# Routing block by block inside the mixer, and new distances between the operands of wide products

## The reference

```
h  = LN0(concat(meta, x))
p  = h @ w_in                  # q,k,v | conv B,C,h | two gates
y  = (g_a * (attention @ w_attn_out) + g_c * (conv @ w_conv_out)) @ w_o
h1 = LN1(alpha*h + y)
g  = top-1 of 4 groups by h1 @ w_rg + b_rg              # softmax over groups
e1, e2 = top-2 of the 8 experts of that group by h1 @ w_re + b_re
weight = g_top * softmax(e_top)
ffn = sum over the 2 experts of weight * (silu(x @ w_gate) * (x @ w_up)) @ w_down
out = LN2(alpha*h1 + ffn)      # meta rows dropped
```

## Time and profile before

| | us |
|---|---|
| median of 3 runs | 4279.54 (4263.64 to 4280.54) |
| profiled execution, its own time | 4267.06 |
| its span | 4265.2 |
| mixer's last wide matmuls end, last router rows begin | about 2634 |
| route, first to last VectorE instruction | 2666.09 to 2744.40 |
| first wide matmul of the experts | 2758.32 |

### The profile page before, as it was taken

One profiled execution on the slowest core, in us unless ns is written; L12 is line 12 of the kernel. 1 busy time (PEld: TensorE's weight loads), 2 busy tenths in 40 slices (PEclk: granted clock), 3 DMA queues, 4 the chain that ended last, 5 costly groups with the idle time before them and its releaser, 6 DMA issues. The chain is left out here.

```text
span 4265.2 us, 60440 instructions
## 1 busy us (share of the span) xinstructions
PE 4144.7 (97%) x20152; PEld 3426.1 (80%) x20153; DVE 2023.0 (47%) x2942; ACT 1433.5 (34%) x2594; POOL 694.2 (16%) x983
## 2 busy tenths in 40 slices
PE   8999999999999999999999998599999999999997
PEld 7888888888888888888888887388788888888886
DVE  3554333433433433433433433677756566765664
ACT  2421311311311311311311310466646465655563
POOL 2000000000000000000000000233333343333333
PEclk9999999999999999999999999799999999999999
DMA  8787355455455455455455454377656566765562
GB/s 249 237 298 244 139 197 211 144 193 209 142 197 204 151 194 197 162 187 194 163 193 190 169 187 178 129 244 253 240 186 217 185 211 224 255 209 194 195 211 90
DMA packets 274310, 839.18 MB, mean 197 GB/s; under 512 B 46128, under 2 KB 95280, under 8 KB 222528
## 3 DMA queue, kind: packets, MB, share of 16 engines
q1 hardware_dynamic: 226080, 715.43, 48.2%
q0 software_dynamic: 48096, 121.71, 8.5%
HBM read 717.47 MB, written 177.21 MB: 210 GB/s over the span
## 5 line engine op out<-in xcount | busy, mean ns | idle before, releaser
L896 PE MATMUL bank<-hT_hi,w_slot 128*128 128x512 f32 x2176 | 861.8, 396 | 7.8 <-DVE w_slot L712 7.1
L897 PE MATMUL bank<-hT_lo,w_slot 128*128 128x512 f32 x2176 | 849.2, 390 | 0.0
L898 PE MATMUL bank<-hT_hi,w_slot 128*128 128x512 f32 x2176 | 848.6, 390 | 0.0
L1652 PE MATMUL e_bank<-e_w_hi,e_xT_hi 128*128 128x512 f32 x1312 | 522.4, 398 | 11.9 <-DVE e_xT_lo L1578 10.6
L1654 PE MATMUL e_bank<-e_w_hi,e_xT_lo 128*128 128x512 f32 x1312 | 514.7, 392 | 0.0
L1653 PE MATMUL e_bank<-e_w_lo,e_xT_hi 128*128 128x512 f32 x1312 | 514.1, 392 | 0.0
L1583 DVE TENSOR_TENSOR e_w_lo<-e_raw,e_w_hi 128x1024 fp32r<-128x1024 f32 x384 | 443.9, 1218 | 118.4 <-ACT e_w_hi L1534 118.4
L896 PEld LDWEIGHTS bank<-hT_hi,w_slot 128*128 128x128 f32 x2176 | 409.0, 188 | 107.2 <-issue 24.1
L898 PEld LDWEIGHTS bank<-hT_hi,w_slot 128*128 128x128 f32 x2176 | 409.0, 188 | 87.3
L897 PEld LDWEIGHTS bank<-hT_lo,w_slot 128*128 128x128 f32 x2176 | 409.3, 188 | 81.8
L1534 ACT ACTIVATE e_w_hi<-e_raw 128x1024 fp32r<-128x1024 f32 x376 | 366.2, 1054 | 0.0
(11 more groups left out here) (275 smaller groups left out, 6496.0 us busy)
## 6 DMA issues: line engine op xcount, KB each, us to landing
w_slot<-split_weights SPq DMA_DIRECT2D x353, 1024.0 KB, 4.8
e_raw<-in_w_exp_gate_dram SPq DMA_DIRECT2D x128, 512.0 KB, 5.9
e_raw<-in_w_exp_up_dram SPq DMA_DIRECT2D x128, 512.0 KB, 6.1
e_raw<-in_w_exp_down_dram SPq DMA_DIRECT2D x128, 512.0 KB, 5.4
split_weights<-w_slot SPq DMA_DIRECT2D x50, 1024.0 KB, 5.9
h_rows<-h_rows SPq DMA_DIRECT2D x64, 512.0 KB, 7.9
x_rows<-in_x_dram SPq DMA_DIRECT2D x32, 512.0 KB, 5.4
raw<-in_w_in_dram SPq DMA_DIRECT2D x30, 512.0 KB, 7.6
```

The source lines that it names most:

```text
L896: pe.matmul(out, hi, x_hi, start=first, stop=False)
L897: pe.matmul(out, hi, x_lo, start=False, stop=False)
L898: return pe.matmul(out, lo, x_hi, start=False, stop=last)
L1652: pe.matmul(out_p, hi, x_hi, start=first, stop=False)
```

## The change

**Routing.** The steps of `route` become functions over 4 tiles (`choose_group`, `choose_first`, `choose_second`, `weigh`, `rank_rows`, `count_up_to`, `place_rows`). In each of blocks 1 to 7 the mixer runs them for the block before, at six places in the strips. GpSimd scatters 8 x 128 records of 8 bytes (row code and weight) into a DRAM tensor `slot_records`, in which every expert has its own region. The tensor is cleared in block 0 by one DMA. After the mixer, `route` does the same for the last block's 4 tiles alone, works out the tile ranges, lists only the last block's 8 x 128 choices by one-hot products, gathers the rest by one indirect DMA of one record row per tile, transposes it and adds the two. Tables (`ident`, `before`, `ones`, `desc`, ...) are made once at the start.

**Distances.** `line_up` puts unused bytes ahead of tensors so that `hT`, `oT`, `zT` and `mixT` start at 256 modulo 512 and `w_slot` at 0. In the experts, 64 unused bytes stand between `e_rows` and `e_xT`, so that `e_xT` and `e_aT` start 64 after `e_w_hi` and `e_w_lo` modulo 512.

```diff
-def mixer(nc, t, x, w_in, w_attn_out, w_conv_out, w_o, h1, logits):
+def mixer(nc, t, x, w_in, w_attn_out, w_conv_out, w_o, h1, tb, records):
...
+        def line_up(name, residue=0):
+            gap = (residue - nc.sbuf_base) % LINE
+            if gap:
+                sb("gap_" + name, [P, gap // 4])
...
+        line_up("hT", HALF)
         hT_hi = sb("hT_hi", [P, KD, TOK], F32R)
...
+        line_up("oT", HALF)
         oT_hi = sb("oT_hi", [P, KA, TOK], F32R)
...
+        line_up("arena", HALF)
+        shared = nc.sbuf_base
         arena = sb("arena", [P, 2 * KD * TOK])
-        weights = -(-nc.sbuf_base // 32) * 32
+        line_up("weights")
+        weights = nc.sbuf_base
...
+        GROUP_AT, FIRST_AT, SECOND_AT, RANK_AT, WEIGH_AT, PLACE_AT = (MIX0 + c for c in (7, 10, 13, 14, 16, 19))
...
+                        if first and s == CONV0:
+                            blanks = 2 * records.shape[0] // P // P
+                            sp.dma_start(records.rearrange("(b p s) c -> p b (s c)", b=blanks, p=P),
+                                         blank[:, :].unsqueeze(1).to_broadcast([P, blanks, P])).then_inc(blank_out, 16)
...
+                    if not first:
+                        hold(po, blank_out, 16)
+                        hold(po, slots_ready, b)
+                        for j in range(2 * TILES):
+                            po.indirect_dma_start(out=records[:, :],
+                                                  out_offset=bass.IndirectOffsetOnAxis(ap=tb["slot"][:, j:j + 1], axis=0),
+                                                  in_=tb["worth"][:, j, :], in_offset=None).then_inc(records_out, 16)
+                        hold(po, records_out, b * (32 * TILES))
+                        po.sem_inc(records_done, 1)
...
+                        if s == SECOND_AT and not first:
+                            a.wait_ge(diff_ready, b)
+                            exponentials(a, r).then_inc(exp_ready, 1)
...
+                        if s == GROUP_AT and not first:
+                            v.wait_ge(lg_taken, b + 1)
+                            choose_group(v, route_link, r, tb)
+                        if s == FIRST_AT and not first:
+                            choose_first(v, route_link, r, tb).then_inc(diff_ready, 1)
+                        if s == SECOND_AT and not first:
+                            choose_second(v, route_link, r, tb).then_inc(both_ready, 1)
+                        if s == WEIGH_AT and not first:
+                            v.wait_ge(exp_ready, b)
+                            v.wait_ge(records_done, b)
+                            weigh(v, route_link, r, tb)
+                            route_link(v.tensor_scalar(tb["token"][:, :], tb["token"][:, :], float(TOK), None, ALU.add))
+                        if s == PLACE_AT and not first:
+                            v.wait_ge(counted, b)
...
+                            place_rows(v, route_link, r, tb, tb["region"]).then_inc(slots_ready, 1)
...
+                        if s == RANK_AT and not first:
+                            pe.wait_ge(both_ready, b)
+                            rank_rows(pe, r, tb, quad[2], E).then_inc(counted, 1)
...
-def route(nc, t, logits, keep, weights):
+def route(nc, t, tb, records, keep, weights):
...
+                po.wait_ge(tile_rows_ready, 1)
+                po.indirect_dma_start(out=got[:, :, :].rearrange("p s c -> p (s c)"), out_offset=None,
+                                      in_=tile_records[:, :],
+                                      in_offset=bass.IndirectOffsetOnAxis(ap=tile_row[:, 0:1], axis=0))\
+                  .then_inc(got_in, 16)
...
-                for j in range(2 * NT):
+                for j in range(2 * TILES):
...
+        sb("e_gap", [P, LINE // 8 // 4])
         xT_hi, xT_lo = sb("e_xT_hi", [P, KD, P], F32R), sb("e_xT_lo", [P, KD, P], F32R)
```

More of the change, by code:

```diff
@@ new lines, in choose_second @@
+def choose_second(v, link, r, tb):
+    EG = r["EG"]
+    first_best(v, link, r, tb, r["inside"][:, :, :], r["best2"], EG, r["place2"], r["tied2"])
+    for hot, place in ((r["hot1"], r["place1"]), (r["hot2"], r["place2"])):
+        ins = v.tensor_tensor(by_group(r, hot[:, :, :]), spread(r),
+                              place[:, :, :].unsqueeze(2).to_broadcast([P, TILES, r["G"], EG]), ALU.mult)
+    link(ins)
+    return v.tensor_tensor(r["both"][:, :, :], r["hot1"][:, :, :], r["hot2"][:, :, :], ALU.add)
@@ new lines, in rank_rows, with count_up_to @@
+def rank_rows(pe, r, tb, bank, E):
+    flat = r["both"][:, :, :].rearrange("p t e -> p (t e)")
+    pe.matmul(bank[:, 0:TILES * E], tb["before"][:, :], flat, start=True, stop=True)
+    return pe.matmul(bank[:, TILES * E:2 * TILES * E], tb["ones"][:, :], flat, start=True, stop=True)
+def count_up_to(v, link, r, tb, totals, E):
+    earlier, base = r["earlier"], tb["base"]
+    link(v.tensor_copy(earlier[:, 0, :], base[:, :]))
+    for q in range(1, TILES):
+        link(v.tensor_tensor(earlier[:, q, :], earlier[:, q - 1, :], totals[:, (q - 1) * E:q * E], ALU.add))
+    link(v.tensor_tensor(base[:, :], earlier[:, TILES - 1, :], totals[:, (TILES - 1) * E:TILES * E], ALU.add))
@@ new lines, in place_rows @@
+def place_rows(v, link, r, tb, starts):
+    E, earlier, slot_f = r["E"], r["earlier"], r["slot_f"]
+    link(v.tensor_tensor(earlier[:, :, :], earlier[:, :, :], starts[:, :].unsqueeze(1).to_broadcast([P, TILES, E]),
+                         ALU.add))
+    for q, hot in enumerate((r["hot1"], r["hot2"])):
+        link(v.tensor_tensor(hot[:, :, :], hot[:, :, :], earlier[:, :, :], ALU.mult))
+        link(v.tensor_reduce(slot_f[:, q, :], hot[:, :, :], AX, ALU.add))
+    return v.tensor_copy(tb["slot"][:, :], slot_f[:, :, :].rearrange("p k t -> p (k t)"))
@@ L195, in mixer @@
         meta_raw = place([weights + 4 * 4 * D], "meta_raw", [P, META_RAW, D])
+        at = [weights + 4 * 8 * D]
+        r = choice_tensors(lambda name, shape: place(at, name, shape), G, E)
         at = [shared]
@@ L973, in block_of_strips @@
                                 pe.wait_ge(lg_taken, b + 1)
+                                if not first:
+                                    pe.wait_ge(ranks_taken, b)
                             for tt in range(TILES):
@@ L1144, in route @@
[L1144 to L1162, removed]
+        upto, first, spare = sb("r_upto", [P, E]), sb("r_first", [P, E]), sb("r_spare", [P, E])
@@ L1202, in _ @@
                 a.wait_ge(diff_ready, 1)
-                a.activation(gexp[:, :, :], gdiff[:, :, :], ACT.Exp).then_inc(exp_ready, 1)
-                a.wait_ge(diff_ready, 2)
-                a.activation(gap_exp[:, :], gap[:, :], ACT.Exp).then_inc(exp_ready, 1)
+                exponentials(a, r).then_inc(exp_ready, 1)
+                for j in range(2 * TILES):
+                    a.wait_ge(hi_made, j + 1)
+                    for q in range(2):
+                        ins = a.activation(listed[:, j, q, :], hot_hi[:, j, :], ACT.Copy,
+                                           scale=tb["worth"][:, j, q:q + 1])
+                    ins.then_inc(worth_made, 1)
                 for c in range(weights["early"]):
@@ L1313, in _ @@
                 v.memset(bounds[:, 2, E - 1:E], MT)
-                v.tensor_scalar(bounds[:, 3, 0:1], upto[:, E - 1:E], -16.0, 16.0 * MT, ALU.mult, ALU.add)
-                v.tensor_scalar(bounds[:, 3, 1:2], upto[:, E - 1:E], -1.0, float(MT), ALU.mult, ALU.add)
                 link(v.tensor_scalar(first[:, :], first[:, :], float(P), None, ALU.mult))
-                for q in range(2):
-                    part = slice(q * half, (q + 1) * half)
-                    link(v.tensor_tensor(earlier[:, part, :], earlier[:, part, :],
-                                         ranks[q][:, :].rearrange("p (t e) -> p t e", e=E), ALU.add))
@@ L1732, in encoder_block @@
                        consts_in=ctx.enter_context(nc.semaphore("e_consts_in")))
-        route(nc, t, logits, keep, weights)
-        experts(nc, t, h1, out2, keep, weights)
+        route(nc, t, tb, records, keep, weights)
+        experts(nc, t, h1, out2, keep, weights, tb)
 _INS = ["x", "meta_tokens", "ln0_g", "ln0_b", "w_in", "attn_sinks", "conv_w", "w_attn_out", "w_conv_out", "w_o",
```

335 lines of the change are left out of this document (170 added, 165 removed).

## The result

The changed kernel takes 4232.64 us (4231.82 to 4235.88, 4 runs) against 4277.01 (4263.64 to 4280.54, 4 runs): ratio 0.9903, 95% interval 0.9881 to 0.9926, 1.0% faster. The forecast was 4145 us, 3.1% faster. The sign and the range (4050 to 4258) held; the size did not. Run again later, it took 4232.07 (6 runs).

What follows compares the result with a forecast made beforehand. The prediction took the mixer as bound by the stream of matmuls, with the route as a hole after it. From the profiled 4267 us, -55 (route), +4 (routing in the mixer) and -72 (distances) gave 4144, stated as 4145; range 4050 to 4258.

Steps and rivals of the forecast that it cites:

- the slow rival: Mixer and experts: new distances act like the 96 bytes or worse; 4346 us at 236 ns, 4284 at 232; 12%.
- Route, -55: Hole between mixer and experts: the route's chain shrinks from 78.3 to 22.9 us, 55 us less, ends -45 and -60.
- The 13.9 us from the route's end to the first wide matmul stay as they are: Between route and experts: ScalarE's splits move behind the listing, VectorE takes the low parts, and the 13.9 us gap stays.
- The records: Route: the gather of records lands 15 to 24 us in, the listing ends at 20, costing nothing or 4 us.
- Routing in the mixer, +4: Mixer: added routing hides in VectorE's idle time and costs 4 us over 7 blocks, ends 0 and +20.
- Distances, -72: Wide matmuls of mixer and experts: both new operand distances give 223 ns from start to start, 72 us less.
- Out strips, -16: Mixer's out strips: 1536 wide matmuls each gain 10.5 ns from the new distance, 16 us less.
- hT and mixT, -32: Mixer's strips on hT and mixT: 8064 wide matmuls each gain 4 ns, 32 us less.
- Experts, -24: Experts: 5928 wide matmuls each gain 4 ns from the 64 byte distance, 24 us less.
- The distances do nothing new: Rival: 256 and 64 bytes act like 0, only the mixer's out strips gain, 10 us; 4206 us; 20%.
- the new distances are worse: Rival on all wide matmuls: they act as the 96 bytes do or worse, 4284 to 4346 us; 12%.
- The lid in the experts: Experts: GpSimd's chain of DMAs, with some 49 us of waits, caps the gain; 24 us fit, 80 wouldn't.

Runs made afterwards that it cites:

- run 2: The changed kernel with the operands where they were before the change, so the new routing alone: 4217.12 us, ratio 0.9871 to the kernel before.
- run 9: The kernel before with oT and zT moved to 0 bytes from the mixer's weights modulo 512, hT from 0 to 256: 4263.31 us, ratio 0.9970.
- run 8: The changed kernel without its 64 byte gap, out strips' products cut to 256 columns on oT and 384 on zT, output left out: 4093.74 us.
- run 3: The kernel before with only 64 unused bytes added between e_rows and e_xT: 4288.72 us, ratio 1.0044.
- run 7: The changed kernel without its 64 byte gap, products on oT using 64 of 128 weight columns, half their output left out: 4181.80 us.

## Why the prediction was wrong in size

The forecast took 132 us off the median, and 44 came, nearly all of it from the route. That the time lies in the range was in part luck: its upper end was added up from unknowns in the mixer, in the route and of the median, and what used the room was mostly the slow rival's effect at 64 bytes, which the range left out.

- **Route, -55:** right in the main. -50.6 measured, -52.6 in run 2. The route came 53.4 us shorter (78.3 to 24.9, forecast 22.9): the listing took 4.4 us for the 4.3 of the estimate, and TensorE's products on it ended 2.0 us after it, where I had 0.9 for start and end. It gave 2.8 back at its end. "The 13.9 us from the route's end to the first wide matmul stay as they are" failed: they are 2701.15 - 2684.48 = 16.7. The traces show what stands there. VectorE was the last engine to end in the route before, and ScalarE's splits ended at 2684.0; now the splits end at 2687.2, 2.7 us after VectorE. From the later of the two it is 13.9 us to the first wide product in both kernels (2758.32 - 2744.40, 2701.15 - 2687.22), and the same in the profiles of all the other versions. So the splits, put behind the listing, set the end of the stage. No run put them elsewhere.
- **The records:** right. The gather, issued at 2670.24, lands in 5.9 us in the DMA view, before the listing's end at 2679.65.
- **Routing in the mixer, +4:** right, 2.4 us in run 2, and 4.8 between the mixer ends of the changed kernel and of run 9. The 6.96 us of the earlier trace rows covered VectorE's pieces: TensorE's waits from 100 to 2630 us, beside the earlier trace rows, are one:

```profile
PE bank L1097 <- DMA w_slot<-split_weights: 0.9, 1, 0.9
```

- **Distances, -72:** this step failed, and it is 80 of the 91 us between 4145 and the profiled 4236. Its sentence was "I take 223 for both new distances: the place acts, ... and I give the move 4 of the 14 ns that are there". Out strips, -16 with 10.5 ns each: 6.6 ns, -10 to -13 us. hT and mixT, -32: nothing. Experts, -24: +19 with the wrong sign. Together +8 instead of -72, and 4267 - 51 + 3 + 8 = 4227 would have been the sum, 9 under the profiled 4236.
- **What was wrong in it.** The trace showed two facts: equal places give 227, 96 bytes give 233. I read the 14 ns between 213 and 227 as more of the 6 between 227 and 233. They are two things: 13 to 14 ns are a fixed price of a product, that run 8 shows at three lengths and none of the places tried takes away; 6 are what the distance decides: no distance of the 16 gets under 226.7. The trace of the kernel before had no row that said a place takes the 14 away, and "equal places let both streams begin together" is a mechanism that no run shows. One might look for the difference at the lower clock. The first products in the experts of the kernel before run at a granted clock of 0.50, which is 1.2 GHz (stretches: us, busy us of the engines, PEclk, DMA share, GB/s; then TensorE in order of time):

```profile
2746.00:2762.00 16.00, 5.62 (x17) 4.48 (x18) 11.96 (x16) 2.48 (x3) 6.21 (x7) 0.50 0.75 269
```

```profile
2758.91 0.63 PE L1653 MATMUL e_bank<-e_w_lo,e_xT_hi 128*128 128x512 f32 x1
2759.34 0.63 PE L1654 MATMUL e_bank<-e_w_hi,e_xT_lo 128*128 128x512 f32 x1
2759.76 0.63 PE L1652 MATMUL e_bank<-e_w_hi,e_xT_hi 128*128 128x512 f32 x1
```

  They start 0.85 / 2 = 425 ns apart, and 512 columns at 1.2 GHz are 427: there the columns' time is reached. The same pair of tensors at the full clock stands 14 ns over it. But at 1.2 GHz a bad place costs nothing either: the changed kernel's first products, with 64 bytes between the same tensors and a granted clock of 0.50 from 2697 to 2703 us, start (2702.59 - 2701.74) / 2 = 425 ns apart too. So both parts show at the faster clock only, and these rows don't part them.
- **The rivals.** "The distances do nothing new" (20%, 4206) was right on 256 bytes and on the out strips (10 us); "the new distances are worse" (12%) was right on 64 bytes, which act "as the 96 bytes do". I gave one fate to both distances. They differ in kind: 256 is half of the 512 by which places are counted, 64 is a fraction like the 96 that the trace had shown to be bad. By a split, 256 as 0 and 64 as 96, the sum from rows of before is 4267 - 55 + 4 - 10 + 5928 x 0.006 = 4242, 6 us from the profile after. Part of that nearness is luck: the 36 us in it for the 64 bytes are 16 to 20 in the medians.
- **The lid in the experts:** I expected GpSimd's chain to cap a gain. There was no gain to cap, so the lid stays untested. GpSimd's waits for the other engines were to shrink, and in sum they did not: 22.8 us for ScalarE, 18.0 for VectorE and 8.8 for TensorE are 49.6, where the earlier trace rows have 16.4, 16.3 and 16.4, which are 49.1. What acted instead was TensorE's own waits, which give back 10 to 13 of 33 us of a loss (run 3). The changed kernel's GpSimd, 2765 to 4180 us:

```profile
POOL e_rstd L1567 <- ACT e_ignored L1622: 22.8, 24, 2.5
...
POOL h_rows L1560 <- DVE e_both L1670: 18.0, 12, 4.2
...
POOL e_x_at L1543 <- PE e_bank L1739: 8.8, 4, 3.8
```

The Trainium skill, "SBUF — State Buffer", section "Who interferes with whom", has TensorE's two read ports independent. The runs here show 226.7 to 234.4 ns by the places of the operands alone, and the measurement decides. By the Trainium skill, "TensorE: Matmul & The Clock Gate", section "Wait — 56ns, not 53.3ns?", a warm product costs some 2.5 ns over its columns, as a fixed price that shows at 2.4 GHz only. The runs here agree with the kind, at both clocks, and not with the size: 13 to 14 ns.

## What to carry to other kernels

An excess over the columns' time has to be split into what differs between two places in the trace and what doesn't before either is priced: here only the first was open to a change of layout. Two edits of one name (here: distances) get one estimate each. A pad of 64 bytes cost 16 to 20 us in this kernel, which is bound by its matmul stream; look at starts of successive products by operand after every change of the allocation. Work that is moved behind the critical chain of a stage can become the stage's end, as ScalarE's splits did here for 2.7 us: ask which engine ends last.

## What the runs showed of the hardware

- At 2.4 GHz the distance of the two operands' starts modulo 256 bytes goes with the time of a product of 128x128 with 128x512 4-byte numbers: 227 ns at 0, 229 at 192, 232 to 233 at 128, 233 to 234 at the rest of the multiples of 32. At 1.2 GHz 64 bytes cost nothing: 427 ns in whole, with them and without.
- Each such product stands 13 to 14 ns over its columns at 2.4 GHz even at 0 or 256 bytes, whatever their number (256, 384, 512), and at 1.2 GHz nothing over them (512 columns: 425 to 427 ns, for 427).
- Half as many stationary columns do not make it shorter (230.6 ns against 227.3, run 7). What the fixed price is, stays open: products that keep their weights, or 2-byte numbers, were not tried.
